# A two-layer decoder trunk on one core: ACT forms the high parts of the streamed weights, GpSimd the low parts

## The reference

```
mod = silu(c) @ w_ada + b_ada            # six rows of 1024: shift, scale, gate for mixing, and for the FFN
h = rmsnorm(x) * (1 + sc_m) + sh_m
proj = h @ w_in                          # gdn q,k,v,z,a,b; ret q,k,v,g; hg q,f,i,g; merge gates
A = gated_delta(silu(conv4(q,k,v)), decay, beta) -> rmsnorm * silu(z)
B = retention(rope(q), rope(k), v)               -> layer norm * silu(g)
C = hgrn2(q, k = 1 - f, v, forget f)             -> rmsnorm * sigmoid(g)
merged = sum_n sigmoid(merge_n) * (branch_n @ w_branch_n)
x = x + gt_m * (merged @ w_out)
h = rmsnorm(x) * (1 + sc_f) + sh_f
x = x + gt_f * ((silu(h @ w_gate) * (h @ w_up)) @ w_down)      # D_FF = 2816
```

## Time and profile before

| | |
|---|---|
| three runs, us | 2747.64, 2752.12, 2753.14 (median 2752.12) |
| the profiled execution | 2748.24 us, span 2746.5 us |
| PE busy | 2536.7 us, 92% of the span |
| DVE busy | 1055.9 us, 38% |
| ACT busy | 442.4 us, 16%, 824 instructions |
| GpSimd busy | 1544.7 us, 56%, 1292 instructions |
| HBM | 95 GB/s over the span, the 16 DMA engines 30% busy |

### The profile page before, as it was taken

The page is one execution under the profiler, slowest core; times in us unless marked ns, Lnnn a source line. Parts: engine busy times, 40 slices in busy tenths (PEclk is TensorE's granted clock), DMA queues, the critical chain, the costliest instruction groups (busy, mean ns, idle before and its releaser), DMA issues. The chain is left out here.

```text
span 2746.5 us, 49611 instructions
## 1 busy us (share of the span) xinstructions
PE 2536.7 (92%) x20358; PEld 2416.3 (88%) x20358; DVE 1055.9 (38%) x1537; ACT 442.4 (16%) x824; POOL 1544.7 (56%) x1292
## 2 busy tenths in 40 slices
PE   4989999999999799999879899999999997999996
PEld 3878998989989799999858799889899796999996
DVE  3564414151743732222146634231427447221222
ACT  2422222121121100000024222310211211000001
POOL 1642235557557677777535322456564585777773
PEclk8999999999999899999979999999999998999998
DMA  8820114223324222322186110142241241223221
GB/s 298 263 91 24 32 39 116 69 66 105 92 59 139 67 78 87 90 88 86 54 320 223 45 32 28 43 123 77 63 135 51 59 150 56 89 85 93 88 86 61
DMA packets 166940, 264.15 MB, mean 96 GB/s; under 512 B 14128, under 2 KB 83248, under 8 KB 164912
## 3 DMA queue, kind: packets, MB, share of 16 engines
q1 hardware_dynamic: 166704, 260.88, 30.3%
HBM read 239.65 MB, written 21.17 MB: 95 GB/s over the span
## 5 line engine op out<-in xcount | busy, mean ns | idle before, releaser
L670 PE MATMUL gemm_psum<-h_hi_lo,w_hi_lo 128*128 128x272 f32 x12000 | 1624.2, 294 | 50.8 <-DVE h_hi_lo L1205 48.7
L670 PEld LDWEIGHTS gemm_psum<-h_hi_lo,w_hi_lo 128*128 128x128 f32 x12000 | 1552.7, 192 | 98.5 <-issue 87.2
L643 POOL TENSOR_TENSOR w_hi_lo<-w_raw,consts 128x512 fp32r<-128x512 f32 (+1 forms) x644 | 683.9, 1062 | 1112.2 <-PE gemm_psum L670 983.7
L645 POOL TENSOR_TENSOR w_hi_lo<-w_raw,w_hi_lo 128x512 fp32r<-128x512 f32 (+1 forms) x644 | 861.5, 1338 | 50.4
L1835 ACT ACTIVATE tiles<-gemm_psum 128x544 f32<-128x544 f32 (+1 forms) x188 | 116.4, 624 | 1185.8 <-PE gemm_psum L670 1185.5
L670 PE MATMUL gemm_psum<-ffn_hi_lo,w_hi_lo 128*128 128x272 f32 x2112 | 265.0, 287 | 0.0
L670 PEld LDWEIGHTS gemm_psum<-ffn_hi_lo,w_hi_lo 128*128 128x128 f32 x2112 | 264.6, 188 | 0.0
L1818 DVE TENSOR_TENSOR tiles<-gemm_psum,tiles 128x544 f32<-128x544 f32 x44 | 31.9, 725 | 389.9 <-PE gemm_psum L670 389.9
L670 PE MATMUL gemm_psum<-o_hi_lo,w_hi_lo 128*128 128x272 f32 x1152 | 153.6, 289 | 0.0
L670 PEld LDWEIGHTS gemm_psum<-o_hi_lo,w_hi_lo 128*128 128x128 f32 x1152 | 146.7, 188 | 0.0
L1835 ACT ACTIVATE scratch<-mix_psum 128x512 f32<-128x512 f32 (+3 forms) x112 | 58.9, 547 | 387.5 <-PE mix_psum L949 176.4
(11 more groups left out here) (233 smaller groups left out, 1982.4 us busy)
## 6 DMA issues: line engine op xcount, KB each, us to landing
w_raw<-in_w_gu SPq DMA_DIRECT2D x176, 256.0 KB, 2.6
tiles<-in_w_ada SPq DMA_DIRECT2D x64, 512.0 KB, 4.5
w_raw<-in_w_merge SPq DMA_DIRECT2D x96, 256.0 KB, 2.6
w_raw<-in_w_first SPq DMA_DIRECT2D x68, 256.0 KB, 5.1
w_raw<-in_w_ret SPq DMA_DIRECT2D x64, 256.0 KB, 2.6
w_raw<-in_w_hg SPq DMA_DIRECT2D x64, 256.0 KB, 2.6
w_raw<-in_w_dn SPq DMA_DIRECT2D x64, 256.0 KB, 2.6
w_raw<-in_w_merge SPq DMA_DIRECT2D x96, 128.0 KB, 2.0
```

The lines of the kernel that those rows point to most:

```text
L643: pool.tensor_tensor(hi, src, ones[:, 0:1].broadcast_to([P, words]), ALU.mult).then_inc(hi_done, 1)
L645: pool.tensor_tensor(lo, src, hi.bitcast(F32), ALU.subtract).then_inc(split_done, 1)
L670: mm = pe.matmul(GP[:, 2 * (tile % 2) + h, 0:HALF], whl[:, n % SLOTS, a, j * P:(j + 1) * P], rhs[:, b, step, h * HALF:(h + 1) * HALF], sta ...
```

## The change

GpSimd's loop keeps one wait and one instruction: the high part's count `hi_done`, then the subtraction. The high parts are formed on ACT, by a copy that writes the rounded format. A new `round_slab` waits, as GpSimd did, for TensorE to be done with slab n - 4 and for slab n to land, then copies and counts `hi_done`. It is called four times behind the copies of adaLN's weights, before `high_parts(0)`. After that ACT's `fill` walks every k-tile of the stream, so its `Feed` begins at tile 0; at each k-tile that ends a slab it calls `round_slab`, for the slab four ahead, and only then evacuates a tile that ends there. Fills are added where ACT had none: behind `high_parts(0)` and in `conv_input`, at the merged products, before the second root, and around the silu tiles of the FFN.

```
--- before.py
+++ after.py
@@ -636,12 +636,8 @@
             def _(pool):
                 for n, (_, _, kt) in enumerate(SLABS):
                     words = kt * P
-                    if n >= SLOTS:
-                        pool.wait_ge(slab_done, n - SLOTS + 1)
-                    pool.wait_ge(landed[n % SLOTS], landed_by[n])
+                    pool.wait_ge(hi_done, n + 1)
                     src, hi, lo = raw[:, n % SLOTS, 0:words], whl[:, n % SLOTS, 0, 0:words], whl[:, n % SLOTS, 1, 0:words]
-                    pool.tensor_tensor(hi, src, ones[:, 0:1].broadcast_to([P, words]), ALU.mult).then_inc(hi_done, 1)
-                    pool.wait_ge(hi_done, n + 1)
                     pool.tensor_tensor(lo, src, hi.bitcast(F32), ALU.subtract).then_inc(split_done, 1)
 
 
@@ -1896,11 +1892,27 @@
                         act.wait_ge(sig("outputs_final"), 2)
                         take(tile, brt[:, HG + i, :], ACT.Sigmoid)
 
-                feed = Feed(CONV_END)
+                feed = Feed(0)
+                rounded = [0]
+
+                def round_slab():
+                    n = rounded[0]
+                    if n == len(SLABS):
+                        return
+                    rounded[0] += 1
+                    words = SLABS[n][2] * P
+                    if n >= SLOTS:
+                        act.wait_ge(slab_done, n - SLOTS + 1)
+                    act.wait_ge(landed[n % SLOTS], landed_by[n])
+                    f(whl[:, n % SLOTS, 0, 0:words], raw[:, n % SLOTS, 0:words], ACT.Copy).then_inc(hi_done, 1)
 
                 def fill(n, limit):
-                    for tile in feed.whole(n, limit):
-                        evacuate(tile)
+                    for tile, step in feed.take(n, limit):
+                        slab, j, kt = TILES[tile][2][step]
+                        if j == kt - 1:
+                            round_slab()
+                        if tile >= CONV_END and step == len(TILES[tile][2]) - 1:
+                            evacuate(tile)
 
                 def drain(limit):
                     fill(10 ** 6, limit)
@@ -1923,7 +1935,10 @@
                 for i in range(2 * KD // ADG):
                     k.next(sig("ada_group_used"))
                     f(ADR[:, i * 4 * P:(i + 1) * 4 * P], B[:, 2 + i % 2, :], ACT.Copy).then_inc(free[2 + i % 2], 1)
+                for _ in range(SLOTS):
+                    round_slab()
                 high_parts(0)
+                fill(KD, CONV_END)
 
 
                 act.wait_ge(sig("conv_landed"), 16)
@@ -2205,16 +2221,22 @@
                 drain(G2_END)
                 for i in range(KD):
                     k.next(sig("merged"))
+                    fill(H, BASE["out"])
                     f(HH[:, 0, i, :], MG[:, i, :], ACT.Copy).then_inc(sig("m_hi"), 1)
 
 
+                drain(BASE["silu0"])
                 k.next(sig("x_sums"))
                 f(halves(RSTD), B[:, 0:2, 0:HALF], ACT.Sqrt, scale=1.0 / D, bias=epsc).then_inc(sig("root_ready"), 1)
                 high_parts(3 * KD)
                 for half in range(2):
                     for i in range(KF):
                         k.next(sig("ffn_slot_free"))
-                        take(BASE[f"silu{half}"] + 2 * i, FT[:, 0, :], ACT.Silu)
+                        tile = BASE[f"silu{half}"] + 2 * i
+                        fill(KD, len(TILES))
+                        take(tile, FT[:, 0, :], ACT.Silu)
+                        fill(KD, len(TILES))
+                    fill(KD * KF, len(TILES))
         clear()
```

## The result

The changed kernel takes 2734.78 us (median of 20 executions, 2722.89 to 2750.85), the one before 2752.38 (20 executions, 2747.54 to 2757.16). The ratio is 0.9938, interval 0.9926 to 0.9949: faster by 17.6 us. Forecast were 2747.8 and a range from 2739 to 2757.5. The direction is right, the size is not: 4.3 us were worked out.

What follows compares the result with a forecast made beforehand. TensorE, busy 92% of the span, was taken to bound the kernel. Gains of 7.2 us and losses of 5.05 us a layer gave -4.3 us for both layers: 2747.8 us against the median, range 2739 to 2757.5.

Steps and rivals of the forecast that it cites:

- What bounds the kernel: Whole kernel: TensorE, busy 92% of the span; GpSimd keeps up everywhere, so unloading it is worth nothing by itself.
- Price of a round: ACT's 128x512 copy forming a slab's high part: 0.65 us each, 644 of them, 419 us, ACT at some 31%.
- Gain 1: Layer's start: four early rounds on ACT leave DVE's modulation undisturbed, first GEMM sooner; 2.7 us a layer.
- Gain 2: Middle norm's modulation: GpSimd silent, so DVE forms low parts unhindered; 1.9 of a 2.04 us wait, each layer.
- Gain 3: Single DVE operations held by GpSimd: four waits of a layer shorter, 1.6 us, and the output GEMM's, 1.0.
- Losses: ACT's rounds delaying evacuations, the first z tile and the roots behind the mixers' outputs: 2.05 + 1.65 + 1.35 = 5.05 us a layer.
- loss 1: Mixers' rope tiles evacuated one round later: +0.6 at the wait of 1.33 at 216.22, together 2.05 us a layer.
- The sum: Both layers: losses 5.05 less gains 7.2, -2.15 us a layer, -4.3 in all, 2747.8 against the median, ±3.
- A: DVE's relief covers ACT's delays: 2742.7 with half of the losses gone, 2737.7 with all; chance 0.24.
- B: Mixers: TensorE waits for ACT's order at 15 or more of 44 other waits, slower, 2760.8 at 20; chance 0.17.
- C: Layer's start: first slabs land too late for ACT's gap, gains equal losses, 2752 ± 2; chance 0.09.

Runs made afterwards that it cites:

- g3: Changed kernel with the FFN's slabs left to GpSimd, which forms both parts there; ratio 0.9955 (0.9934 to 0.9976) to the kernel before.
- h1: Kernel before with ACT rounding only the mixers' slabs, first rope tile to last branch tile; ratio 0.9978 (0.9957 to 0.9999) to the kernel before.
- f3_warm_mid: Changed kernel with 80 further matmuls on TensorE while it waits for the middle norm; ratio 0.9929 (0.9906 to 0.9953) to the kernel before.

## Why the prediction was wrong

- **What bounds the kernel:** right. TensorE's waits in the four traces name neither GpSimd nor a slab, and in the FFN it does 401 or 402 matmuls in 50 us as before.
- **Price of a round:** right, 0.632 us for 0.65, ACT 822 us for some 860.
- **Gain 1:** right in waits (TensorE at 59.34, forecast 59.2). TensorE's waits for the normalized tiles fell from 48.7 and 50.9 to 41.2 and 38.7 us, with gain 2; 2 x (2.7 + 1.9) = 9.2 were worked out. In time the part alone gave nothing that could be told (from 3.6 us faster to 2.2 slower).
- **Gain 2:** right, 2.1 to 3.1 us a layer by g3.
- **Gain 3:** near for the waits that were named (L698 to L694, 11.5 to 9.4, for four waits of some 0.4; the output GEMM's waits of 1.9 are gone), but incomplete. Other waits behind DVE in the mixers got shorter too: L892 to L888, 7.4 to 6.5; L694 behind the other releaser, 11.0 to 9.6, of which 0.9 came back as a wait for ACT; L930 behind DVE, 8.4 and 7.8 to 4.7, 6.0 and 6.1. These 3 to 5 us weren't in the sum.
- **Losses:** near as sizes, with one exception. L930 waits for ACT 5.4 instead of 1.0 us, +4.4 (2 x (0.65 + 1.65) = 4.6); L942 to L938 6.6 to 8.0, +1.4 (1.6); L920 to L916 3.9 to 7.6 in one trace pair and 6.4 to 7.7 in another (1.2), where the wait of 1.33 at 216.22 became 3.26 by itself (+1.9 for the +0.6 of loss 1); the squares' L720 +3.7, of which L729 gives back 3.0 in one trace pair and 1.1 in another (2.7). With GpSimd kept busy the mixers' waits rose by 9.5 us for the 10.1, but 3.8 of that is one wait that no loss named (L892, 7.4 to 11.2).
- **The sum:** this step failed. It is a sum of waits: -4.3 us, and -6.8 is measured in idle time. But it was set equal to the time, which fell by 17.6. It put TensorE's busy time at no change, without a reason, although the trace of the kernel before had a mean granted clock of 0.959, and 0.96 over layer 1's mixers (columns as in the windows above):

```profile
180.00:865.00 685.00, 646.44 (x5036) 613.91 (x5037) 265.56 (x446) 127.53 (x220) 324.40 (x270) 0.96 0.23 66
```

  What the runs show in its place: 6.8 us of the 17.6 are idle time, and the rest, some 11 us, came as busy time at a higher mean granted clock (0.9590 to 0.9614 and more; 4 to 11 us by the slopes, 6.0 us less busy time in the mean of the four traces). In the mixers the sum had +7.7; h1 measures -6 (-11.8 to -0.3), with idle time up by 1 us and busy time down by 5 to 8. Why the clock rose stays open.
- **The rivals:** A, more relief, comes nearest in time (2737.7 with all losses gone; measured 2734.8), but that is luck in part: the losses are there, and busy time made up for them. B didn't occur: the mixers' waits rose by 5 us in all, and not by 9.8 and more on top of the losses. C didn't: the slabs had landed. The rule of the Trainium skill (ScalarE: Activation LUTs, "What ACT_TABLE_LOAD costs"), a drain on top of each table load, is not borne out: the z tile's evacuation begins 0.01 us behind the load's end.

## What to carry to other kernels

Where work is moved off GpSimd, count first whom its instructions hold up: here DVE had lost 136 us beside products that read SBUF, and this time of DVE's, not GpSimd's own, is what paid. A sum of waits is a forecast of TensorE's idle time, not of the time; where TensorE works between short chains at a mean granted clock that isn't 1.0 (0.96 here), its busy time needs a term of its own, and several traces of either kernel to see it. And undoing a known loss isn't a gain by itself: the evacuation put first took 3 us of waits away and brought 7 others.

## What was not expected of the hardware

- Executions of the changed kernel spread over 28 us (2722.89 to 2750.85), with a mean granted clock of 0.955 to 0.967; its four traces, 19 us apart, have the same idle time within 3 us. The kernel before spread over 10 us.
- A DVE addition of 128x32 takes 192 ns beside a GpSimd that only writes and 776 to 811 on average beside one that reads.
- DVE's conversions with one input are held as well: in the FFN the cast of 128x544 takes 1234 ns in the changed kernel, 486 with the product kept. There the subtraction behind it is the one that meets GpSimd's low part (1.70 us at 1102.80, 0.73 in the changed kernel).
- At the middle norm 17 to 20 us at half clock cost 0.5 us at most (f3_warm_mid).
